# Issuing the value loads of a decoder step's attention from ScalarE's queue

## The reference, cut to what matters

```python
x = LN1(alpha*x + 0.5*gate1 * SwiGLU_1(mod1(x)))
h = mod2(x); q, k, v of both mixers = split(h @ w_qkv)
x = LN2(alpha*x + gate2 * ([mixA(h) ; mixB(h)] @ w_o))
x = LN3(alpha*x + 0.5*gate3 * SwiGLU_2(mod3(x)))

# mixer A: 8 heads x 64, windows (128,1), (512,4), (2048,16) over the cached
# window plus the new rows, merged by their softmax denominators
# mixer B: 4 heads, q and k in two halves of 64, v of 128, keys and values
# gathered from pages:
past_k = pool_k[page_table]; past_v = pool_v[page_table]     # 16 pages of 128
o = softmax(q1 k1) v - lambda * softmax(q2 k2) v             # RMSNorm per head
```

## Time and profile before

| what | value |
|---|---|
| median of 3 runs | 1682.48 us (1680.62 to 1684.63) |
| profiled execution, its own time | 1686.0 us |
| its span, first to last instruction | 1684.2 us |
| busy: PE, PEld, DVE, ACT, POOL | 91%, 80%, 40%, 31%, 4% |
| granted clock of TensorE, mean | 0.958 |
| attention | about 711 to 1150 us of the span |
| moved by DMA | 245.71 MB, mean 146 GB/s |

### The profile page before, as it was taken

The page is one execution under the profiler, slowest core; times in us unless marked ns, Lnnn a source line. Parts: engine busy times, 40 slices in busy tenths (PEclk is TensorE's granted clock), DMA queues, the critical chain, the costliest instruction groups (busy, mean ns, idle before and its releaser), DMA issues.

```text
span 1684.2 us, 31988 instructions
## 1 busy us (share of the span) xinstructions
PE 1534.2 (91%) x12575; PEld 1341.7 (80%) x12575; DVE 667.2 (40%) x1333; ACT 513.7 (31%) x835; POOL 66.1 (4%) x162
## 2 busy tenths in 40 slices
PE   4899999999998999888898878877899999999996
PEld 3788999999996777655565555547789999999996
DVE  0322323322426423354554545645643232332343
ACT  2411222221214121244444444443342222221122
POOL 0200000000002000000000000000010000000000
PEclk9999999999998999989999999988989999999998
DMA  9993232232222141478888998873212222233211
GB/s 331 389 333 123 75 87 78 84 99 86 72 71 83 50 131 63 123 218 264 264 264 270 256 273 246 271 228 96 73 45 81 87 75 87 77 99 86 85 54 57
DMA packets 215906, 245.71 MB, mean 146 GB/s; under 512 B 9023, under 2 KB 152889, under 8 KB 215810
## 3 DMA queue, kind: packets, MB, share of 16 engines
q1 hardware_dynamic: 215810, 244.42, 46.9%
HBM read 237.31 MB, written 7.08 MB: 145 GB/s over the span
## 4 chain that ended last, share of the span: by engine, by line
PE 40%; SPq 8%; issue 3%; DMA 3%; DVE 3%; ACT 2%; ACTq 0%; DVEq 0%
PE ps L288 27%; SPq L1170 4%; SPq L1147 4%; PE ps L1256 3%; DMA kv<-in_cache_diff_k_dram 3%; PE ps L272 2%; PE ps L1268 1%; PE ps L1312 1%; PE ps L1330 1%; PE ps L952 1%; PE ps L1355 1%; PE ps L1295 1%; DVE VH L1571 1%; DVE xT L312 1%; DMA kv<-in_cache_win_v_dram 0%
## 5 line engine op out<-in xcount | busy, mean ns | idle before, releaser
L257 ACT ACTIVATE whi<-w 128x1024 fp32r<-128x1024 f32 (+1 forms) x152 | 171.1, 1128 | 741.5 <-PE ps L288 641.9
L263 DVE TENSOR_TENSOR wlo<-w,whi 128x1024 fp32r<-128x1024 f32 (+1 forms) x152 | 200.4, 1319 | 422.3 <-ACT whi L257 422.0
L288 PE MATMUL ps<-hhi,whi 128*128 128x288 f32 x1440 | 310.7, 297 | 3.7 <-ACT tmp L653 3.7
L288 PE MATMUL ps<-hlo,whi 128*128 128x288 f32 x1440 | 308.9, 296 | 0.0
L288 PE MATMUL ps<-hhi,wlo 128*128 128x288 f32 x1440 | 308.7, 296 | 0.0
L288 PEld LDWEIGHTS ps<-hhi,whi 128*128 128x128 f32 x1440 | 232.2, 189 | 9.2 <-issue 4.8
L288 PEld LDWEIGHTS ps<-hlo,whi 128*128 128x128 f32 x1440 | 232.8, 189 | 0.0
L288 PEld LDWEIGHTS ps<-hhi,wlo 128*128 128x128 f32 x1440 | 232.5, 189 | 0.0
L1256 PEld LDWEIGHTS ps<-ident,kv 128*128 128x128 f32 (+1 forms) x896 | 101.7, 149 | 88.9 <-issue 65.4
L1256 PE MATMUL ps<-ident,kv 128*128 128x128 f32 (+1 forms) x896 | 126.1, 283 | 46.0 <-DMA kv<-in_cache_diff_k_dram 33.2
L288 PE MATMUL ps<-ffhi,whi 128*128 128x288 f32 x704 | 151.2, 296 | 0.0
(11 more groups left out here) (197 smaller groups left out, 1684.8 us busy)
## 6 DMA issues: line engine op xcount, KB each, us to landing
w<-in_ffn_w_in_dram SPq DMA_DIRECT2D x88, 512.0 KB, 3.8
wada<-in_w_ada_dram SPq DMA_DIRECT2D x18, 2048.0 KB, 13.8
kv<-in_cache_diff_k_dram SPq DMA_DIRECT2D x128, 256.0 KB, 4.0
kv<-in_cache_diff_v_dram SPq DMA_DIRECT2D x128, 256.0 KB, 3.6
w<-in_ffn_w_out_dram SPq DMA_DIRECT2D x32, 704.0 KB, 4.6
w<-in_w_qkv_dram SPq DMA_DIRECT2D x24, 512.0 KB, 3.7
kv<-in_cache_win_k_dram SPq DMA_DIRECT2D x32, 384.0 KB, 5.1
kv<-in_cache_win_v_dram SPq DMA_DIRECT2D x32, 384.0 KB, 7.6
```

Source lines behind the costliest of these rows:

```text
L257: nc.scalar.activation(whi[:, slot, 0:w], w32[:, slot, 0:w], ACT.Copy).then_inc(ph.hi, 1)
L263: nc.vector.tensor_tensor(wlo[:, slot, 0:w], w32[:, slot, 0:w], whi[:, slot, 0:w].bitcast(F32), ALU.subtract).then_inc(ph.lo, 1)
L288: m = pe.matmul(ps[:, banks + h, 0:TH], w, x[:, kk, h * TH:(h + 1) * TH], start=(kk == 0 and n == 0), stop=(kk == kall - 1 and n == 2))
```

## The change

`attend_loads` now takes the engine as an argument and is called twice: SP gets a `load` for keys, ACT one for values. SP's row loses the value loads. ACT issues a value load in each quarter between `copy_weights` and `prompt_exp`, for the chunk of 4 quarters ago (`LAG - 1`), that is, one quarter before its product. Before the sequences, ACT also waits for the end of the `w_qkv` products.

```diff
-        def attend_loads():
-            eng = nc.sync
+        def attend_loads(eng):
...
-                    vb, vi = back(b, i, LAG)
-                    if alive(vb):
-                        load(vb, vi, 1)
-
             each_sequence(body)
...
             eng = nc.scalar
+            load = attend_loads(eng)
...
                     if alive(lb) and li % 4 == 0:
                         copy_weights(lb, li, True)
+                    vb, vi = back(b, i, LAG - 1)
+                    if alive(vb):
+                        load(vb, vi, 1)
                     if alive(b):
                         prompt_exp(b, i, mixer_of(b, run))
                         evacuate(b, i, 2)
...
             for g in (1, 4):
                 eng.wait_ge(sem(f"kept{g}"), 16 * (PT_ + 1))
+            eng.wait_ge(qkv.used, 24)
             over_sequences(eng, body)
...
-            load = attend_loads()
+            load = attend_loads(sp)
```

## The result

The changed kernel takes 1802.28 us (1800.77 to 1804.81, 4 runs) against 1683.56 us of the kernel before on the same chip (1680.62 to 1684.85, 4 runs): ratio 1.0709, 95% interval 1.0684 to 1.0734, 118.7 us slower. The forecast was 1799 us, 117 us slower. The profiled execution has a span of 1799.0 us against 1684.2.

The account below looks back on a forecast made before the run. In attention no engine is full; keys come late because values stand before them in the sync queue's row. Terms 109 + 9 + 12 + 8 + 18 - 39 = 117 us gave 1799 us, range 1725 to 1875.

Parts of the forecast that it names:

- The group on ACT: In quarters 0 to 3 of sequences 1 to 7, four value page reads and issues on ACT take 4.7 us.
- Its price: The group delays exponential, copy of keys and scores by 3.9 us in each of 28 quarters: 109 us.
- The clock: New PE gaps in attention lower its granted clock: 20 more gaps at 0.9 us, 18 us (bounds 0 and 73).
- rival 3: In attention, late values and the lower clock add up, both bounds reached by half or more: about 1865 us; 13%.
- PE's page waits: In attention, all of PE's waits for pages of keys and values go: 38.6 us gained (bounds 0 and 38.6).
- Values that land late: Value loads land after PE is ready for their product: 0.4 us in each of 32 quarters, 12 us (bounds 0, 48).
- Mixer A's values on ACT: In quarters 4 and 5 of 8 sequences, two DMAs on ACT cost 0.55 us each quarter, 9 us; quarters 6, 7 covered.
- The drain: At attention's end, the last page groups on ACT delay copies of weights and the square of the prompt's norm: 8 us.
- Rival 1: ACT's queue runs ahead, page groups fit into ACT's idle time, only the gain is left: 1650 us; 8%.
- Rival 2: The group is cheap on ACT: no change at 1.6 us, 1690 to 1745 us at 2 to 3.5; 12%.
- Rival 4: Keys and values from two issuers slow each other, the 39 us aren't gained: about 1838 us; counted in the forecast's spread.
- what would have shown it: Quarters 0 to 3 about 4 us longer, copy-of-keys wait over 90, page-key wait near 0, DMA about 0.75, clock below 0.94.

## Why the prediction was right

The forecast was within 4 us of the measured time, and its mechanism is what the trace shows. That it came so close is luck: the term of the clock was three times too small, and the others made up for it.

- **The group on ACT: right.** Forecast 4.7 us, seen 4.50 to 4.84. Eight reads without a DMA give nearly the same loss (112 us), four issues without reads a small one.
- **Its price: a little high.** Forecast 3.9 us in each of 28 quarters, 109 us; measured 93.8 us of added waits for the copy of keys, of which 91.5 (97.9 less 6.4) from the second sequence to the drain, 3.3 us each. Part of a group lies beside what PE still had in its row, and that work was slower than before, which likely is the difference; no run takes it apart.
- **The clock: the mis-sized term.** Forecast 18 us (bounds 0 and 73), measured +53.9 us of busy PE for the same matmuls. I priced each gap as one slow group of transposes, from the one gap of the earlier trace rows. In the page quarters of sequence 3 the gaps repeat every 10 to 12 us, and much of what lies between them runs slow too: 27.15 us instead of 19.95 for 254 matmuls, at a granted 0.77 instead of 1.00. That was one half of rival 3, which I had put at 13%. Filling the gap returned 36 us net.
- **PE's page waits: right in kind.** Forecast -39, measured -32.9 for keys; the 5.4 us for value pages in the quarters went too, but the drain brought 6.6.
- **Values that land late: wrong.** Forecast 12 us. In the stretch from 762 to 1225 us PE's list of waits has no row for values; the 2.8 us are in the first sequence and the 6.6 in the drain. I had counted 0.4 us in hand, with the product 8.7 us after the copy of weights. In sequence 3 the product of quarter 3 came 11.5 us after the copy of quarter 2 (925.34, 936.86), while the last of its pages, issued at 929.5, landed at most 5.0 us later: over 2 us in hand. Likely the slower PE delays the product beyond the group; no run tries that by itself. The one kernel whose quarters were short, with fixed page numbers, did wait 30.6 us.
- **Mixer A's values on ACT:** forecast 9 us, not seen apart: quarters 4 to 7 of sequence 3 fell from 30.7 to 26.3 us with them in it, and PE's scores of quarters 4 and 5 there (948.88, 954.89) waited for nothing. The first sequence, which has only these and no pages on ACT, became about 4 us longer, 2.8 of them a wait for its values.
- **The drain: right in size.** Forecast 8 us, measured 8.3 (35.1 to 43.4). The path was another: 5.8 us of it is PE's wait for the pages of the third group, rather than the square of the norm.
- **Sum.** The measured parts are 93.8 + 53.9 - 32.9 + 3.8 - 3.0 = 115.6 us. Against the forecast the clock is 36 us over, keys 6 us; the group is 15 us under, late values 8, mixer A's values 9 and the drain 8, since neither needs a term beside the waits, and the small waits 3. The total was better than its parts.

Rival 1, that ScalarE's queue runs ahead, is out: in sequences 3 and 4 each page group starts within 0.3 us of the copy of weights, and eight reads in that place cost 112 us. The Trainium skill's lifecycle ("Perfetto Trace Analysis", on DVE and ACT instructions), by which the queue would have gone on, is not borne out where the wait is unfulfilled. The clearest place is quarter 2 of sequence 4, whose program is written out: the queue executed its last separate wait at 989.4, ACT then idled until the copy of weights at 990.45, and the first page read started at 990.5. It does pass an activation that stands only behind ACT's own work: in quarter 1 of sequence 3 the reads started at 913.1, the second copy of weights at 913.38. The Trainium skill's sentence that issuing is small relative to the DMA ("DMA: Bandwidth & Descriptors", "Issuing engines are not separate DMA queues") isn't either for page groups: reading four page numbers and issuing four DMAs is 4.5 us against 4.1 to landing. Rival 2 fell with the length of the group. Rival 4 has no part in this result (the wait for keys went), but what it names is real: it ate the gain of the kernel that moved only mixer A's values.

Of what would have shown it, all held in kind: page quarters longer with the wait ended by the copy of keys (over 90, measured 104.7), wait for keys near 0, quarters 4 to 7 shorter (by 4.4, expected 6), clock below 0.94 (0.83). The DMA share went below the forecast, 0.66 instead of 0.75. The page quarters grew by 5.4 us each instead of 4: 1.8 us of it is slower matmuls, (27.15 - 19.95) / 4.

## What to carry to other kernels

Before moving DMA issues to a compute engine, count what the issuing sequencer does for them, register reads included, and what stands behind them on that engine: time in its queue is paid in large part (here 3.3 us for a group of some 4.6) if the next instruction is one that the bottleneck waits for. First shorten the row where it stands: page numbers read once and used for keys and values gave 1.35%, and reading them in quarters where the sync queue was free 2.05% in all, while the move cost 7.1%. And price a repeated gap of TensorE by what it does to the clock of all the work around it, not by its length.

## What the runs showed of the hardware

- **The clock's cost is not in proportion to the gap.** The kernel before, with eleven waits for keys of up to 5.2 us, had a granted clock of 0.94 in attention. With waits of up to 2.2 us for the copy of keys (four reads) it was 0.96, with waits of up to 4.2 us (eight reads) 0.85, and with the gap filled 0.99. Busy PE in attention was 306.4, 351.9 and, with more matmuls, 383.2 us. Together with the key waits that a delay gives back this makes the second four reads cost 99 us where the first four cost 13: the first gave back 26.7 us of key waits, and only 6.5 were left to give.
- **Two hardware queues don't keep each other's order.** At the place shown, with values issued 0.2 us after pages of keys on the other queue, the last page landed after 8.6 us; with them 0.4 us after on the same queue, after 5.0. It is a comparison of one place in two traces.
- **ScalarE's queue is serial with the wait ahead of it.** Page reads began with the copy of weights in quarter 2 (925.4 and 925.34), after 1.00 us in which ACT was idle; in sequence 4 the same (990.5 and 990.45), after 0.71 us.
